# Sums of squares for the second norm: first four tiles added up by TensorE in its bank, last four by VectorE

## What is computed

```python
def _rmsnorm(x, g):
    xf = x.astype(F32)
    y = xf * lax.rsqrt(jnp.mean(xf * xf, axis=-1, keepdims=True) + EPS) * g.astype(F32)
...
        h = _rmsnorm(x, norm_mix[layer])
        mix, hg_s = _hgrn2(h, layer, hg_s, hg_w_in, hg_lower_bounds, hg_out_gain, hg_w_out)
        x = x + mix.astype(x.dtype)
        x = x + _swiglu(_rmsnorm(x, norm_ffn[layer]), ffn_w_gu[layer], ffn_w_down[layer])
```

## Time and profile before

| | us |
|---|---|
| median of 3 runs | 2622.48 |
| lowest, highest of these | 2621.48, 2627.33 |
| the profiled execution, its own time | 2628.2 |
| its span, from first to last instruction | 2626.5 |
| TensorE busy in it | 2566.9 (98%) |
| VectorE busy | 1757.3 (67%) |
| ScalarE busy | 1236.1 (47%) |
| mean granted TensorE clock | 0.994 |

### The profile page before, as it was taken

One profiled execution on the slowest core, in us unless ns is written; L12 is line 12 of the kernel. 1 busy time (PEld: TensorE's weight loads), 2 busy tenths in 40 slices (PEclk: granted clock), 3 DMA queues, 4 the chain that ended last, 5 costly groups with the idle time before them and its releaser, 6 DMA issues.

```text
span 2626.5 us, 52531 instructions
## 1 busy us (share of the span) xinstructions
PE 2566.9 (98%) x16420; PEld 2341.2 (89%) x16420; DVE 1757.3 (67%) x2989; ACT 1236.1 (47%) x2195; POOL 225.9 (9%) x224
## 2 busy tenths in 40 slices
PE   8999989999999999999999999999999999999998
PEld 7999989999998887999987888899997888799897
DVE  5555587877756667666666666766565666776565
ACT  5444454443444555443435555534344555644343
POOL 4111000000011120000002120000002121000001
PEclk9999999999999999999999999999999999999999
DMA  5221345645443223665653222667454222467574
GB/s 185 97 60 56 113 145 169 215 158 183 164 147 85 75 76 117 221 204 172 209 163 99 75 78 87 209 183 229 152 180 150 73 79 73 157 195 224 156 224 144
DMA packets 203409, 379.66 MB, mean 145 GB/s; under 512 B 23168, under 2 KB 23200, under 8 KB 203056
## 3 DMA queue, kind: packets, MB, share of 16 engines
q1 hardware_dynamic: 202896, 369.73, 44.9%
q0 software_dynamic: 384, 8.44, 0.9%
HBM read 331.67 MB, written 52.74 MB: 146 GB/s over the span
## 4 chain that ended last, share of the span: by engine, by line
PE 69%; DVE 2%; issue 2%; ACT 2%; DMA 1%; SPq 0%; ACTq 0%; DVEq 0%; POOL 0%; POOLq 0%
PE ps L453 12%; PE ps L455 12%; PE ps L454 12%; PE ps L545 8%; PE ps L546 8%; PE ps L547 8%; PE ps_s L331 1%; PE ps_s L547 1%; PE ps_s L545 1%; PE ps_s L546 1%; PE ps_o L371 1%; DMA w_raw<-w_all 1%; PE ps_u L356 1%; PE ps_o L366 1%; ACT w_hi L773 0%
## 5 line engine op out<-in xcount | busy, mean ns | idle before, releaser
L545 PE MATMUL ps<-h,g_hi 128*128 128x256 f32 (+1 forms) x2112 | 608.6, 288 | 26.9 <-DVE ebuf L1263 8.6
L546 PE MATMUL ps<-h,g_hi 128*128 128x256 f32 (+1 forms) x2112 | 604.6, 286 | 0.0
L547 PE MATMUL ps<-h,g_lo 128*128 128x256 f32 (+1 forms) x2112 | 604.5, 286 | 0.0
L953 DVE TENSOR_TENSOR w_lo<-w_raw,w_hi 128x512 fp32r<-128x512 f32 x512 | 361.0, 708 | 256.0 <-ACT w_hi L773 254.3
L453 PE MATMUL ps<-h_hi,w_hi 128*128 128x512 f32 (+1 forms) x1280 | 470.5, 368 | 16.0 <-DVE h_lo L958 10.6
L773 ACT ACTIVATE w_hi<-w_raw 128x512 fp32r<-128x512 f32 x512 | 317.2, 624 | 326.9 <-PE ps L455 309.0
L454 PE MATMUL ps<-h_lo,w_hi 128*128 128x512 f32 (+1 forms) x1280 | 451.9, 353 | 0.0
L455 PE MATMUL ps<-h_hi,w_lo 128*128 128x512 f32 (+1 forms) x1280 | 451.6, 353 | 0.0
L545 PEld LDWEIGHTS ps<-h,g_hi 128*128 128x128 f32 x2112 | 402.0, 190 | 36.9 <-DVE ebuf L1263 15.0
L453 PE MATMUL ps<-a_hi,w_hi 128*128 128x512 f32 (+1 forms) x1200 | 428.5, 357 | 5.1 <-DVE a_lo L1021 2.5
L454 PE MATMUL ps<-a_lo,w_hi 128*128 128x512 f32 (+1 forms) x1200 | 422.6, 352 | 0.0
(11 more groups left out here) (182 smaller groups left out, 3518.4 us busy)
## 6 DMA issues: line engine op xcount, KB each, us to landing
w_raw<-w_all SPq DMA_DIRECT2D x516, 256.0 KB, 2.6
g_raw<-w_all SPq DMA_DIRECT2D x286, 256.0 KB, 3.4
g_x<-kept_sum SPq DMA_DIRECT2D x132, 256.0 KB, 3.5
g_hi<-kept_hi SPq DMA_DIRECT2D x132, 256.0 KB, 2.8
g_lo<-kept_lo SPq DMA_DIRECT2D x132, 256.0 KB, 3.0
kept_sum<-g_x SPq DMA_DIRECT2D x44, 256.0 KB, 3.0
kept_hi<-g_hi SPq DMA_DIRECT2D x44, 256.0 KB, 2.5
kept_lo<-g_lo SPq DMA_DIRECT2D x44, 256.0 KB, 2.7
```

The source lines that it names most:

```text
L545: pe.matmul(out, g_hi[:, o, k, :].bitcast(F32R), hh, start=(k == 0 and not more), stop=False, skip_group_check=True)
L546: pe.matmul(out, g_hi[:, o, k, :].bitcast(F32R), hl, start=False, stop=False, skip_group_check=True)
L547: mm = pe.matmul(out, g_lo[:, o, k, :].bitcast(F32R), hh, start=False, stop=last, skip_group_check=True)
L953: nc.vector.tensor_tensor(w_lo[:, r, :, :], w_raw[:, r, :, :], w_hi[:, r, :, :].bitcast(F32), ALU.subtract).then_inc(w_lo_ready, 1)
```

## The change

Tiles are counted d = 0..7 in the order in which w_out finishes them.

- Squares of tiles 0 to 3 all go to ebuf[d % 2], and TensorE adds them up: `square_sum` multiplies the matrix of ones by the square, in float32, into the norm's bank (ps_o, and ps_k in block 0), where the sums stay until `norm_sum` adds the rest. One `square_sum` stands behind every second piece of w_out's pairs 2 and 3: tile 0's behind pair 2's piece n = 1, tile 1's behind n = 3, tile 2's and tile 3's likewise in pair 3.
- The square of tile 4 goes to ssq. VectorE adds those of tiles 5, 6 and 7 to it, so three adds stand where seven stood.
- `norm_sum` of this norm adds to the bank (start=False) where it began it anew.
- ScalarE's waits before the squares: tiles 2 and 3 wait for the `square_sum` of tiles 0 and 1; tile 5 waits for the `square_sum` of tile 3, tile 6 for that of tile 2, and tile 7 for VectorE's add of tile 5. Tile 4 waits for none of these.

```diff
+BY_TENSOR = 4
...
+    sq_summed = sem("sq_summed")
...
-            def norm_sum(b, T, nth):
+            def norm_sum(b, T, nth, begun=False):
...
-                    mm = pe.matmul((ps_o if bank == 0 else ps_k)[:, 0:n], ones[:], ssq[:, c:c + n], start=True, stop=True)
+                    mm = pe.matmul((ps_o if bank == 0 else ps_k)[:, 0:n], ones[:], ssq[:, c:c + n], start=not begun, stop=True)
                 mm.then_inc(xms_ready, 1)
+
+            def square_sum(b, T, d):
+                pe.wait_ge(xsq_ready, KT * (2 * b + 1) + d + 1)
+                pe.sem_inc(passed)
+                for bank, c, n in halves(T):
+                    mm = pe.matmul((ps_o if bank == 0 else ps_k)[:, 0:n], ones[:], ebuf[:, d % 2, c:c + n], start=(d == 0), stop=False)
+                mm.then_inc(sq_summed, 1)
...
                     piece(b, T, slot(b, 2 * (i % 2) + m),
                           OUT0 + 2 * P_OUT * i + n, n, half, KT, a_hi, a_lo)
+                    if i >= 2 and n % 2 == 1:
+                        square_sum(b, T, 2 * (i - 2) + n // 2)
...
-                    norm_sum(b, T, 2 * b + 1)
+                    norm_sum(b, T, 2 * b + 1, True)
...
                 act.wait_ge(xms_ready, nth)
-                if d > 2:
-                    act.wait_ge(ssq_ready, (KT + 1) * nth + d)
+                if d in (2, 3):
+                    act.wait_ge(sq_summed, BY_TENSOR * b + d - 1)
+                elif d in (5, 6):
+                    act.wait_ge(sq_summed, BY_TENSOR * b + (4 if d == 5 else 3))
+                elif d == 7:
+                    act.wait_ge(ssq_ready, (KT + 1) * nth + 3)
                 act.sem_inc(passed)
-                to = ssq[:, 0:T] if d == 0 else ebuf[:, d % 2, 0:T]
+                to = ssq[:, 0:T] if d == BY_TENSOR else ebuf[:, d % 2, 0:T]
...
                 nth = 2 * b + 1
-                if d == 0:
+                if d <= BY_TENSOR:
                     return
                 dve.wait_ge(xsq_ready, KT * nth + d + 1)
-                if d > 1:
-                    dve.wait_ge(ssq_ready, (KT + 1) * nth + d + 1)
-                nc.vector.tensor_tensor(ssq[:, 0:T], ssq[:, 0:T], ebuf[:, d % 2, 0:T], ALU.add).then_inc(ssq_ready, 3 if d == 1 else 1)
+                wait(dve, ssq_ready, (KT + 1) * nth + 3 * (d - BY_TENSOR - 1))
+                nc.vector.tensor_tensor(ssq[:, 0:T], ssq[:, 0:T], ebuf[:, d % 2, 0:T], ALU.add).then_inc(ssq_ready, 3)
```

## The result

The changed kernel took 2649.57 us (median of 6 runs, 2647.54 to 2651.25); the kernel before, on the same chip, 2624.74 us (6 runs, 2621.48 to 2627.33). The ratio is 1.0093, with a 95% interval of 1.0083 to 1.0104: 24.8 us slower. The forecast was 2640.1 us, 17.6 us more, and its range ended at 2649. The direction was right; the time is 7 us more than forecast (against the new median of before) and just outside the range. The profiled execution took 2651.25 us itself, with a span of 2649.5 us.

The account below looks back on a forecast made before the run. TensorE was taken to bound the kernel, with gaps ended by late VectorE. Block 0's 9.1 us plus 8.5 us for blocks 1 to 3 made 17.6 us on 2622.5: 2640.1 us, range 2630 to 2649.

Parts of the forecast that it names:

- What bounds the kernel: TensorE, busy 98% of the span; late VectorE makes it wait 8.5 us in six waits in blocks 1 to 3.
- part 1: Four of seven adds leave VectorE in each block: 2.4 us a block, tile 6 that much earlier if taken alone.
- both waits of rows 3: TensorE's waits in block 2 for tile 6 (1.79 us) and tile 7 (1.04 us) to leave their banks.
- Part 2: Each square_sum costs TensorE 0.87 us, or 0.98 us in block 0; 14.4 us more work in all.
- Part 3: ScalarE's square of tile 5 waits for square_sum 3, so tile 6 comes 2.82 us later; blocks 1 to 3: 8.5 us.
- rival 3: Blocks 1 to 3: shorter waits keep TensorE at 2.4 GHz, -3.1 us in sum, 2637 us; chance 0.2.
- Block 0: Tile 5's square waits for square_sum 3, delaying tile 6 and A22's low part: +9.1 us.
- Square_sum 3 starts at 355.34 + 3 x 0.98 = 358.28: Block 0: start of the last square_sum, from gate_up's old start plus three square_sums; tile 5's square then starts at 359.47.
- all of it is over before tile 5's, which sets the date anew: Block 2: tile 3's square waits for square_sum 1, costing ScalarE 1.9 us, said to end before tile 5's wait.
- Rival 4: Weight pieces split behind tile 3's square come late for w_out, TensorE stands: 7.6 us more, 2647.7 us; chance 0.1.
- The clock in block 0: Opposite of rival 3: a slow clock after longer waits in block 0 would cost some 1.5 us.

Follow-up runs that it names:

- four buffers: Changed kernel with the squares of tiles 2, 3 and 7 in fbuf, so ScalarE waits for no square_sum: 2625.10 us, 0.9997 to the kernel before.
- the second trace: Changed kernel run once more, nothing altered, for its ratio and another trace: 2649.18 us, 1.0088 to the kernel before.
- four buffers in blocks 1 to 3: Changed kernel with block 0 as in the kernel before, and elsewhere squares in ebuf and fbuf without ScalarE waits for square_sum: 2621.03 us, 0.9984.
- the version with two tiles: Block 0 as before; in blocks 1 to 3 TensorE sums only the squares of tiles 0 and 1, VectorE makes five adds: 2620.42 us, 0.9983.

## Why the prediction was right or wrong

- **What bounds the kernel, and part 1**: right in the main. The lighter VectorE is worth 7.6 us by itself, and nothing of it is left once ScalarE stands. Of "both waits of rows 3 would vanish" only tile 6's did; tile 7's of 1.04 us stayed.
- **Part 2, the price of a `square_sum`**: right, 0.92 us against 0.87 in blocks 1 to 3, 0.95 against 0.98 in block 0 (7.35 us from one to the next with four buffers, less 6.4 for 48 matmuls). That it is no full term of its own holds: 14.4 us of such work cost 3.2 by themselves, 6.8 beside the relief.
- **Part 3, ScalarE's waits in blocks 1 to 3**: right, mechanism and sum. 8.5 us forecast, 9.2 measured with block 0 put back (5.5 to 12.6 by the interval). The trace gives less, 0.7 + 2.7 + 2.2 us. Block 1's 0.7 is set against a clock of 0.93 in the one trace of before; 0.98 and 1.00 in the changed kernel have the shape of rival 3, but the measured time shows no saving. Block 2's 2.7 is the forecast's 2.8 partly by luck: an early `square_sum` and a slow stretch cancel, and the second trace has 4.0.
- **Block 0**: here is the error. The failed step is "Square_sum 3 starts at 355.34 + 3 x 0.98 = 358.28". It takes w_out to run through. The sentence on tile 3's wait, "all of it is over before tile 5's, which sets the date anew", was worked out in block 2, where a tile of w_out has one of four slots, and was carried over to block 0, which has two. There tile 3's wait delays tile 4's eviction, tile 6 needs tile 4's slot, and TensorE stands for 3.36 us; the slow clock behind it adds 1.7 us in the one trace. The last `square_sum` is 5 us late, and so is all that hangs on it. With the waits of tiles 2 and 3 taken away the wait of w_out is gone from the trace and the chain has the prediction's 9.1 us; the measured time falls by 2.6 to 3.9 us, which by itself is at the edge of the noise. With only tile 5's taken away the 3.36 us stay. So the block made some 14 to 15 us where the sum had 9.1.
- **Rival 4** had the shape of it (TensorE itself stands, both waits feed each other), but with another carrier: the weight pieces. They didn't come late; it was a bank. Its chance of 0.1 and a range that left out its far end were too little.
- **The clock in block 0**: "some 1.5 us" was named for a slow stretch after longer waits and left out of the sum. The traces show 1.7, 3.0 and 4.0 us behind single waits. Not all of it lasts to the end of the block (last section).
- **The range** was built from rivals, each alone; block 0's slot wait and the clock add up. With the slot wait and the clock in the sum, by hindsight, 17.6 + 3.4 + 1.5 = 22.5 us would have been forecast.

## What to carry to other kernels

Before a wait on one engine is called harmless, follow it to every resource that the engines behind it free, in each variant of the loop: here the wait for tile 3's buffer (2.4 us) left w_out running where it has four slots, and stopped TensorE for 3.4 us where it has two. A wait that hides behind a longer one can come to light when that one is removed: tile 3's cost 1.1 us in each of blocks 1 to 3 once tile 5's was gone. When work moves to an engine that runs behind, the buffers that it reads stay taken for as long as it lags, so count them first; here two more buffers undid the loss. Where a change pays in one variant of the loop only, make it there only.

## What the runs showed of the hardware that was not expected

A wait of TensorE of the same length can be followed by a slow stretch or not. A22's wait in block 0 was 2.83 us in the kernel before and the clock stayed at full speed up to the norm's sum. Three versions have the same code in block 0 and the same wait of 2.83 us. With block 0 as before and blocks 1 to 3 as changed, it went as in the kernel before; with four buffers in blocks 1 to 3 the clock was 1.00 from 360 to 380, with no slow stretch at all; in the version with two tiles the wait was followed by 9 us at half speed (1.2 GHz):

```profile
363.00:366.00 3.00, 2.95 (x12) 0.50 0.55 173
366.00:369.00 3.00, 2.45 (x11) 0.50 0.32 89
369.00:372.00 3.00, 3.00 (x14) 0.50 0.21 37
```

Its norm's sum was 3.9 us later than before, yet 0.7 us were left of that at block 1's head 0. In the kernel before a slow stretch comes a few us later instead, at 372 to 375, where the clock is 0.51. So a position read inside block 0 is uncertain by up to 4 us from one execution to the next, and only what is left at the block's end, or the medians of several runs, should be set against a sum. The rule of the Trainium skill, page "TensorE: Matmul & The Clock Gate", section "Part 1: The HAM clock gate (the "warmup" mystery)", that the throttled clock is the default and activity releases it, fits block 1, where the waits for tiles 6 and 7 were 1.78 and 1.03 us at a clock of 0.93 in the kernel before, and 1.35 and 1.05 us at 0.98 and 1.00 in the changed kernel's two traces. That is one trace against two, and no test of the rule. Which of two equal waits is followed by a slow stretch, it does not tell, and no run here shows why.

What a slow stretch costs depends on the wait behind it. In the version with block 0 as before and blocks 1 to 3 as changed, block 2 has a slow stretch ahead of the wait for ScalarE's copy (granted clock 0.57 from 1662 to 1666) and block 3 has none (1.00 from 2279 to 2287); the wait is 0.63 us in one and 1.73 in the other, and gate_up's first matmul to the norm's sum takes only 0.4 us more in block 2. In the changed kernel's first trace the slow stretch of block 2 (0.57 as well) lies behind that wait, and the same distance is 1.5 us longer than in block 3, where there is none.
